# A decoder trunk's second router tile: residual and transposes in halves, one-hot straight from PSUM, and expert buffers refilled by halves

## What is computed

```python
x = x + merged @ w_out[l]
x = x + hierarchical_moe(rms_norm(x, ffn_norm[l]), ...)

def hierarchical_moe(x, wg, bg, we, be, w_gate, w_up, w_down):
    g_logits = xt @ wg + bg                  # 4 groups
    grp = argmax(g_logits)                   # top-1 group
    e_logits = (xt @ we + be)[tok, grp]      # its 8 experts
    top_p, top_i = top_k(softmax(e_logits), 2)
    weights = p_grp * top_p / sum(top_p)
    ...
    h = silu(xt @ w_gate[e]) * (xt @ w_up[e])    # 32 experts, 1024 -> 256
    y += (h * combine[:, e]) @ w_down[e]         # 256 -> 1024
```

## Time and profile before

| | before |
|---|---|
| median of 3 runs | 464.75 us |
| the profiled execution, its own time | 465.2 us |
| its span, first to last instruction | 463.5 us |
| TensorE busy | 408.9 us (88%) |
| VectorE busy | 216.8 us (47%) |
| ScalarE busy | 173.6 us (37%) |
| GpSimd busy | 39.8 us (9%) |
| bytes moved by DMA | 146.79 MB, 317 GB/s over the span |

### The profile page before, as it was taken

One profiled execution on the slowest core, in us unless ns is written; L12 is line 12 of the kernel. 1 busy time (PEld: TensorE's weight loads), 2 busy tenths in 40 slices (PEclk: granted clock), 3 DMA queues, 4 the chain that ended last, 5 costly groups with the idle time before them and its releaser, 6 DMA issues.

```text
span 463.5 us, 6606 instructions
## 1 busy us (share of the span) xinstructions
PE 408.9 (88%) x2697; PEld 290.5 (63%) x2697; DVE 216.8 (47%) x332; ACT 173.6 (37%) x269; POOL 39.8 (9%) x66
## 2 busy tenths in 40 slices
PE   1999999999999999999999899999929669299686
PEld 1789999999878787888888753535502414125122
DVE  3676997487899994573584640211100101002011
ACT  4547529963665374244356331110201001002001
POOL 8420291000000000000002100000000000000000
PEclk9999999999999999999999999999979969789799
DMA  8988793455552468798489999999999999999993
GB/s 295 349 254 284 257 393 105 166 182 181 182 181 93 182 216 329 255 411 287 181 322 378 393 343 426 424 421 418 429 422 422 423 420 430 420 413 415 412 411 146
DMA packets 40987, 146.79 MB, mean 317 GB/s; under 512 B 2715, under 2 KB 4368, under 8 KB 31616
## 3 DMA queue, kind: packets, MB, share of 16 engines
q1 hardware_dynamic: 39360, 143.24, 79.8%
q10 hardware_dynamic: 848, 2.62, 1.7%
q0 software_dynamic: 752, 0.55, 0.6%
HBM read 145.35 MB, written 1.05 MB: 316 GB/s over the span
## 4 chain that ended last, share of the span: by engine, by line
PE 63%; DMA 20%; SPq 10%; DVE 3%; ACT 2%; issue 1%; DVEq 0%
PE psum L1597 19%; DMA ring<-in_exp_w_down 14%; PE psum L1593 13%; PE psum L1803 7%; PE psum L1853 5%; DMA a_att<-in_exp_w_down 5%; SPq L409 4%; PE psum L2065 4%; PE psum L1974 3%; SPq L457 2%; PE psum L1943 2%; SPq L425 1%; PE psum L1695 1%; PE psum L1775 1%; DMA tok<-in_x 1%; SPq L414 1%
## 5 line engine op out<-in xcount | busy, mean ns | idle before, releaser
L1064 DVE TENSOR_TENSOR wl<-ring,wh 128x2048 fp32r<-128x2048 f32 (+1 forms) x38 | 85.0, 2244 | 36.0 <-ACT wh L743 35.9
L743 ACT CAST wh<-ring 128x2048 fp32r<-128x2048 f32 (+1 forms) x38 | 71.1, 1870 | 56.0 <-PE psum L1597 20.9
L1597 PE MATMUL psum<-wh,x_parts 128*128 128x512 f32 (+1 forms) x288 | 66.2, 382 | 0.2 <-ACT a_att L852 0.2
L1535 DVE COPY mix<-psum 128x512 f32<-128x512 f32 (+1 forms) x8 | 5.3, 658 | 116.9 <-PE psum L2065 111.5
L1597 PEld LDWEIGHTS psum<-wh,x_parts 128*128 128x128 f32 x288 | 52.2, 189 | 10.6 <-issue 0.4
L1010 ACT COPY mix<-psum 128x512 f32<-128x512 f32 x8 | 4.7, 586 | 105.3 <-PE psum L2065 101.3
L1974 PE MATMUL psum<-a_att,mix 128*32 128x512 f32 x96 | 25.2, 684 | 18.3 <-DMA a_rnn<-in_exp_w_up 17.4
L1593 PE MATMUL psum<-x_parts,wh 128*128 128x256 f32 x320 | 40.5, 284 | 0.0
L1593 PEld LDWEIGHTS psum<-x_parts,wh 128*128 128x128 f32 x320 | 39.1, 192 | 0.1
L1597 PE MATMUL psum<-wl,x_parts 128*128 128x512 f32 (+1 forms) x144 | 34.1, 379 | 0.3 <-DVE wl L1064 0.3
L2065 PE MATMUL psum<-ring,a_moe 128*32 128x512 f32 x152 | 28.2, 676 | 6.4 <-DMA ring<-in_exp_w_down 6.4
(11 more groups left out here) (308 smaller groups left out, 596.7 us busy)
## 6 DMA issues: line engine op xcount, KB each, us to landing
ring<-in_w_in SPq DMA_DIRECT2D x12, 2048.0 KB, 7.8
ring<-in_exp_w_down SPq DMA_DIRECT2D x19, 1024.0 KB, 16.4
odd<-in_exp_w_gate SPq DMA_DIRECT2D x12, 1024.0 KB, 15.3
odd<-in_exp_w_up SPq DMA_DIRECT2D x12, 1024.0 KB, 17.3
a_att<-in_exp_w_gate SPq DMA_DIRECT2D x8, 1024.0 KB, 15.0
a_att<-in_exp_w_up SPq DMA_DIRECT2D x8, 1024.0 KB, 17.0
mix<-in_exp_w_down SPq DMA_DIRECT2D x6, 1024.0 KB, 27.0
a_rnn<-in_exp_w_gate SPq DMA_DIRECT2D x4, 1024.0 KB, 21.4
```

Of the source, the lines that this page charges most:

```text
L743: a.copy(high, src).then_inc(hi_ready, 1)
L1064: signal(v.tensor_tensor(low, src, halves(m, wh)[1].bitcast(fp32), ALU.subtract), lo_ready, m + 1)
L1597: ins = t_.matmul(bank(name)[:, 0:n], xp[hf][:, k, i * P:(i + 1) * P], wv[:, k, :], start=start, stop=stop)
```

## The change

It touches four things.

1. **The last residual.** VectorE adds bank "wo3" in two halves of 256 columns. TensorE turns each half into a bank of its own (5 and 7) in `turn_x1_last`; ScalarE copies the first, VectorE the second. `logits(1, 0)` moves ahead of these transposes, and the triangle product of tile 0 behind them. `pos_ps[0]` moves from bank 5 to bank 4.
2. **The pick chain.** `gkey` is now made with -`NEG` (1e30) times the group's descending number, so that subtracting its maximum gives the bar directly: one instruction in place of two in `picks`.
3. **The one-hot.** The triangle has -1024 on its diagonal and `iot` counts from -1024, so a picked token's place can be compared as it stands in PSUM. The instruction that made `pos1` is taken out from ahead of the one-hot; a copy (`kept_places`) takes its place, in front of the one-hot for tile 0 and behind it for tile 1.
4. **The first refills.** `gate_up_first` multiplies gate and up apart (256 columns a matmul instead of 512), gate first; after each half it adds 1 to `first_pairs`, and SyncE refills each 1 MB half on its own count (`gate_up_halves`).

GpSimd gets two more setup instructions, VectorE one.

```diff
-        pos_ps = [psum[:, 5 + 2 * t, 0:E] for t in range(TT)]
+        pos_ps = [psum[:, 4, 2 * E:3 * E], psum[:, 7, 0:E]]
...
+            def gate_up_halves(g, j):
+                dst = even[j].rearrange("p (m n) -> p m n", m=2)
+                for m, w in enumerate((wg_v, wu_v)):
+                    n = 2 * FIRST.index(j) + m + 1
+                    if n < 2 * NDOUBLE:
+                        sp.wait_ge(first_pairs, n)
+                    else:
+                        sp.wait_ge(kpair_done, 4)
+                    sp.dma_start(dst[:, m], w[g][:, j, :]).then_inc(even_full[j], 16)
...
                     if g == 1:
-                        sp.wait_ge(kpair_done, FIRST.index(j) + 1)
+                        gate_up_halves(g + 1, j)
...
+            step(g.affine_select(out=tri[:], in_=tri[:], compare_op=ALU.not_equal, fill=-float(FAR), base=0,
+                                 pattern=[[1, P]], channel_multiplier=-1))
-            step(g.iota(iot[:], pattern=[[1, SLOTS]], base=1, channel_multiplier=0, ...
+            step(g.iota(iot[:], pattern=[[1, SLOTS]], base=-FAR, channel_multiplier=0, ...
+            step(g.iota(gdesc[:], pattern=[[-1, 4]], base=4, channel_multiplier=0, ...
...
             x2_copy(2)
+            act.wait_ge(turn_full, 4 + 4)
+            a.copy(x2T[:, 4:6, P:2 * P], psum[:, 5, 0:2 * P]...).then_inc(x2T_copied, 1)
             squares(3)
...
+            do(v.tensor_scalar(gdesc[:], gdesc[:], -NEG, None, ALU.mult))
...
             def picks(t):
-                chain(v.tensor_scalar(gbar[:, t, :], gkey[:, t, :], rs[:, 2, t:t + 1], NEG, ALU.not_equal, ALU.mult))
-                chain(v.tensor_tensor(el5[:, t, :]..., lg[:, t, 4:KR]..., bc(gbar[:, t, :]...), ALU.add))
+                chain(v.scalar_tensor_tensor(el5[:, t, :]..., bc(gkey[:, t, :]...), rs[:, 2, t:t + 1],
+                                             lg[:, t, 4:KR]..., ALU.subtract, ALU.add))
...
             def first_hot(t, done, value):
                 dve.wait_ge(pos_done, t + 1)
-                chain(v.scalar_tensor_tensor(pos1[:, t, :], pos_ps[t], 1.0, A[:, t, :], ALU.add, ALU.mult))
                 signal(v.tensor_tensor(hot[:, t], bc(iot[:].unsqueeze(1), [P, EG, SLOTS]),
-                                       bc(pos1[:, t, 0:EG].unsqueeze(2), ...), ALU.is_equal), done, value)
+                                       bc(pos_ps[t][:, 0:EG].unsqueeze(2), ...), ALU.is_equal), done, value)
+            def kept_places(t):
+                do(v.tensor_copy(pos1[:, t, :], pos_ps[t]))
...
-            residual(3)
+            full(dve, "wo3")
+            last_rows = x1[:, 1, CB:]
+            v.tensor_tensor(last_rows[:, 0:2 * P], ..., bank("wo3")[:, 0:2 * P], ALU.add).then_inc(x1_half, 1)
+            free(v.tensor_tensor(last_rows[:, 2 * P:], ..., bank("wo3")[:, 2 * P:], ALU.add), "wo3")
             mean2(1)
+            dve.wait_ge(turn_full, 4 + 5)
+            v.tensor_copy(x2T[:, 6:8, P:2 * P], psum[:, 7, 0:2 * P]...).then_inc(x2T_last, 1)
+            dve.wait_ge(pos_done, 1)
+            kept_places(0)
             first_hot(0, hot_t0, 1)
-            dve.wait_ge(turn_full, 4 + 4)
-            v.tensor_copy(x2T[:, 4:8, P:2 * P], psum[:, 7, :]...).then_inc(x2T_last, 1)
             rstd2(1)
             groups(1)
             picks(1)
             first_hot(1, hot_ready, 1)
+            kept_places(1)
...
                     pe.wait_ge(even_full[j], 32)
-                    for k in range(2):
-                        for e in range(EG):
-                            ins = t_.matmul(h_ps[e * SLOTS:(e + 1) * SLOTS, :]..., xg[...], w[:, e, k], ...
-                    ins.then_inc(kpair_done, 1)
+                    for m in range(2):
+                        for k in range(2):
+                            for e in range(EG):
+                                ins = t_.matmul(h_ps[e * SLOTS:(e + 1) * SLOTS, m * F:(m + 1) * F], xg[...], ...
+                        if n == NDOUBLE - 1 and m == 1:
+                            ins.then_inc(kpair_done, 4)
+                        else:
+                            ins.then_inc(first_pairs, 1)
```

More of the change, by code:

```diff
@@ L985, in _ @@
             x2_copy(2)
+            act.wait_ge(turn_full, 4 + 4)
+            a.copy(x2T[:, 4:6, P:2 * P], psum[:, 5, 0:2 * P].rearrange("p (a b) -> p a b", a=2)).then_inc(x2T_copied, 1)
             squares(3)
@@ L1629, in turn_x1, with turn_x1_last @@
                 turn_free(i, x1[:, i // 2, i % 2 * CB:(i % 2 + 1) * CB])
+            def turn_x1_last():
+                src = x1[:, 1, CB:]
+                for k in range(4):
+                    if k == 0:
+                        pe.wait_ge(x1_half, 1)
+                    if k == 2:
+                        wait_freed("wo3")
+                    ins = t_.transpose(psum[:, 5 + k // 2 * 2, k % 2 * P:(k % 2 + 1) * P], src[:, k * P:(k + 1) * P],
+                                       ident[:, :])
+                    if k % 2:
+                        ins.then_inc(turn_full, 1)
             split_block("q", turned="xT")
@@ L1904, in _ @@
             out_pass("wo1", 1, 1, 1)
+            logits(1, 0)
+            turn_x1_last()
             pe.wait_ge(picks_ready, 1)
             t_.matmul(pos_ps[0], tri[:, :], A[:, 0, :], start=True, stop=True).then_inc(pos_done, 1)
-            turn_x1(3)
-            logits(1, 0)
             logits(1, 1)
@@ L1955, in gate_up_first @@
                     pe.wait_ge(even_full[j], 32)
-                    w = even[j].rearrange("p (m e k f) -> p e k m f", m=2, e=EG, k=2)
-                    for k in range(2):
-                        for e in range(EG):
-                            ins = t_.matmul(h_ps[e * SLOTS:(e + 1) * SLOTS, :].rearrange("p (m f) -> p m f", m=2),
-                                            xg[:, 2 * j + k, e * SLOTS:(e + 1) * SLOTS], w[:, e, k],
-                                            start=(n == 0 and k == 0), stop=(n == 3 and k == 1),
-                                            skip_group_check=True)
-                    ins.then_inc(kpair_done, 1)
+                    w = even[j].rearrange("p (m e k f) -> p m e k f", m=2, e=EG, k=2)
+                    for m in range(2):
+                        for k in range(2):
+                            for e in range(EG):
+                                ins = t_.matmul(h_ps[e * SLOTS:(e + 1) * SLOTS, m * F:(m + 1) * F],
+                                                xg[:, 2 * j + k, e * SLOTS:(e + 1) * SLOTS], w[:, m, e, k],
+                                                start=(n == 0 and k == 0 and m == 0), stop=(n == 3 and k == 1),
+                                                skip_group_check=True)
+                        if n == NDOUBLE - 1 and m == 1:
+                            ins.then_inc(kpair_done, 4)
+                        else:
+                            ins.then_inc(first_pairs, 1)
             def gate_up(odd_group, nth):
```

29 lines of the change are left out of this document (18 added, 11 removed).

## The result

The changed kernel is slower. Its median is 466.98 us over 19 runs (465.24 to 469.13), that of the kernel before, beside it on the same chip, 465.43 us (464.67 to 467.64); the ratio of the times is 1.0034, 95% interval 1.0023 to 1.0046. Forecast were 463.35 us and "faster" with a chance of 0.72. In a second comparison the same kernel came out at 1.0015 (1.0006 to 1.0025). The profiled execution took 468.2 us, of which 464.8 are the recorded span, from the first to the last instruction (before: 465.2 and 463.5).

The account below looks back on a forecast made before the run. Full DMA engines were taken to bound the kernel from 264 us; an earlier first refill (0.4 - 0.1 + 0.2 + 0.2 + 0.86 = 1.56) closes a 1.4 us break: 464.75 - 1.4 = 463.35 us, range 462.6 to 464.6.

Parts of the forecast that it names:

- The rest: Added setup on GpSimd and the extra VectorE instruction lie under TensorE's unbroken 258 us; nothing charged.
- slower: Rival: the doubled first pass starves the next refill near 286 us; net +3.5, 468.2 us; chance 0.04.
- three signs: Wrong if flow breaks near 289, rates fall below 415 after 300, or the first refill goes out after 267.8.
- Halved residual and copies: Ahead of the second tile's logits: narrower copies and earlier transposes win 0.4 us (0.27 to 0.54).
- GpSimd's hold: GpSimd's last product may delay a VectorE instruction of tile 1; cost 0 to 0.57 us, taken as 0.1.
- Pick chain: In the router's picks, one instruction takes the place of several; wins 0.2 us (0.1 to 0.26).
- one-hot: Router's one-hot reads PSUM directly, so the 0.23 us step ahead of it goes; wins 0.2 us.
- refills by halves: First gate-and-up buffer: its first half is free after 0.86 us instead of 1.72; wins 0.86 (0 to 0.86).
- From S to time: Transfer break at 268.5 to 271.0 us: a first refill 1.56 earlier closes it, winning 1.4 us.
- S: How much earlier the first refill is issued: 1.56 us, at 267.15 instead of 268.71; bounds -0.1 to 1.9.
- more than the break: Rival: uneven flow after the restart, beyond 271 us, goes too; 0.5 more won, 462.85 us; chance 0.07.
- A break later on: After the eight refills, near 289 us: 2.0 us spare before the next transfer, so no break opens.

Follow-up runs that it names:

- before_shift32: Kernel before plus an unused 32-byte tensor in the place of `gdesc`, nothing else changed; 466.99 us against 465.12, ratio 1.0041.
- after_small_router: Changed kernel with `gdesc` in free columns of `small` (old addresses) and the first refills whole as before; 464.69 us, ratio 0.9998 to the kernel before.
- after_small: Changed kernel with `gdesc` kept in free columns of `small`, so every address is that of the kernel before; 464.93 us, ratio 0.9995 to the kernel before.
- after_small_base128: Changed kernel with `gdesc` in `small`, and every tensor moved up by 128 bytes together; 463.88 us, ratio 0.998 to the kernel before.

## Why the prediction was wrong, point by point

**The failed step is "The rest": "Nothing is charged".** I counted the setup's instructions and overlooked that one of them had to write somewhere. `gdesc` was costed as work and not as bytes. Its 32 bytes cost 1.85 us of span (`before_shift32`). Of these, 0.6 come by `product`: its 144 matmuls take 0.9 longer, the first 0.3 of which are gone in a wait behind them (the transposes that follow the first third end at 156.0 in both), and the last `out_pass` of that kernel starts at 257.06, not 256.47. The bytes that flow from 268 to 454 make about 0.8, and 0.4 single profiles don't place. No rival had this, nor a mechanism near it. The chance of 0.05 for "slower" was meant for another mechanism, so that the sign was among the cases at all is luck. None of the three signs that the prediction gave for being wrong came: no break near 289, 417 GB/s from 300 to 453, the first refill at 267.77. They watch the change's own mechanism, and the loss came from beside it.

**Not in the sum either: 0.25 to 0.3 us outside the recorded span.** They follow the router part (1.98 in `after_small_router`), not the halves (1.79), the bytes (1.73), the semaphores (1.75) or the setup (1.73); these are medians. Which of the router's instructions makes them, and how, stays open.

**Halved residual and copies, GpSimd's hold.** Right. Seen from the late end of `out_pass`, `groups(1)` gains 0.35 (261.32 against 260.98, with 0.69 of delay); forecast 0.4 - 0.1. GpSimd's product runs from 260.52 to 261.80, and the instruction that it might have held starts at 261.81 and takes 0.22: not held.

**Pick chain, one-hot, refills by halves.** Right in size: from the start of `groups(1)` to the end of `picks(1)` 2.50 instead of 2.69, from there to the one-hot 0.50 instead of 0.73, and 0.83 for the halves by themselves.

**From S to time.** Too high with the old addresses. With S = 1.65 the span fell by 0.9 there; with the shifted ones, at S = 1.63, by the 1.4 that was forecast. The difference of these two is no larger than their scatter. The stretch from 268 to 277, first the kernel before, then `after_small`:

```profile
268.00:277.00 9.00, 8.72 (x80) 4.31 (x73) 4.97 (x22) 2.55 (x8) 0.00 (x0) 1.00 0.88 325
```

```profile
268.00:277.00 9.00, 8.76 (x128) 6.30 (x121) 4.72 (x21) 2.25 (x3) 0.00 (x0) 1.00 0.97 388
```

At 422 GB/s, (1 - rate / 422) x 9 us is lost here: 2.1 and 0.7. Over the profiles of the nine kernels without either part it is 1.3 to 2.6, 2.0 in the mean, and of the five with the whole change 0.5 to 1.2, 0.8 in the mean. So the flow after a restart can stay uneven up to 277, as the rival "more than the break" supposed, but the change does not remove all of it. With the halves alone the loss is 0.9 and 1.3, with the router part alone 0.7. The spans read 0.65 and 0.60 less for the parts by themselves and 0.9 for both. Both series suggest that the first 0.8 of S buys most and the second finds less left; it isn't shown, since the differences are as large as the scatter.

**A break later on.** Right: the next set is issued at 286.15, and the rate is unbroken. The pass with twice the matmuls takes 7.12 us, against 7.07 in the kernel before, by the start of its first matmul and the end of its last; the rival "slower" did not occur. The 1.7 us that the prediction estimates for weight loads in the open did not come either.

**The numbers together.** The bytes by themselves cost 1.85 (`before_shift32`), the change at the old addresses wins 0.9 of span and loses 0.3 outside (`after_small`): +1.85 - 0.9 + 0.3 = +1.25. Measured were +0.65 in the second comparison and +1.55 in the first, one below and one above. (The 1.4 won against the shifted layout can't be used here, since it is taken from the second comparison itself.) The interval of the first (1.0023 to 1.0046) and that of the second (1.0006 to 1.0025) touch only just. The distance lies in the span, 464.7 against 463.85 for the same kernel, and I have no cause for it.

## What to carry to other kernels

A new tensor is an edit to every tensor declared behind it: put it at the end or into unused columns, and compare the rows of untouched code (mean ns of one, bytes in a fixed stretch) before crediting or blaming the edit. If they have moved, run the kernel before with a pad of the same size; that one run tells layout from work. Read the addresses out of the built kernel before you reason about them: one run here tested the reverse of what it was meant to. Where transfers set the pace, a few common shifts of all tensors are worth a try: here one took 1.2 us off the span, where the whole change took 0.9.

## What the runs showed of the hardware that I had not expected

- A 128x512 matmul of `product` takes 389 to 391 ns or 395 to 397 ns by where its two operands lie: shifts of one against the other by 32, 64 or 128 bytes are slow, by 0 or 256 fast.
- The rate of 16 full DMA engines goes by the addresses of the tensors filled: over 100 us 421 GB/s with none of them on a multiple of 256 bytes, 422 to 423 with one, 426 to 427 with all but one. Within a kernel it differs by destination: 428 while `a_att` is filled on a multiple of 256, 418 on the same stretch with `a_att` 128 bytes higher. The same place ran at 426 to 427 when the other tensors stood on multiples of 256, and the rule behind that stays open.
- The time outside the span isn't constant between kernels: 1.7 us or 2.0 in the median, in single executions up to 4.3 (`after_small_base128`).
